# One layer of a hybrid decoder: the attention heads taken by pairs, on halves of TensorE's rows and columns

## The reference, cut to what matters

```
xn   = RMSNorm(x)
proj = xn @ w_in     -> q, k, v (8 heads of 64), index q (8 x 64), index k (64), index w (8), u (256), qm (4 x 64)
A    = sparse attention: index score = sum over 8 heads of relu(iq . ik / 8) * iw, causal;
       the 64 best keys of each query are kept; softmax(q . k / 8) over them, times v
B    = pooling mixer: causal windows 2, 4, 8, 16 over 4 groups of 64 channels, each group times its 64 x 64 weight
C    = cross-attention of qm (4 heads of 64) into 256 memory tokens
h    = x + (sum over branches of sigmoid(xn @ w_gate + b_gate) * (branch @ w_proj)) @ w_out
h    = h + MoE(RMSNorm(h)): the best 4 of 32 experts, clamped SwiGLU, 1024 -> 2048 -> 1024
out  = RMSNorm(h)
```

## Time and profile before

| | us |
|---|---|
| median of 3 runs (lowest, highest) | 1206.98 (1204.16, 1207.64) |
| profiled execution, its own time | 1203.21 |
| its span, first to last instruction | 1201.0 |
| PE busy in the span | 1121.9 (93%) |
| DVE busy | 359.7 (30%) |
| ACT busy | 227.3 (19%) |
| POOL busy | 128.6 (11%) |

### The profile page before, as it was taken

One profiled execution on the slowest core, in us unless ns is written; L12 is line 12 of the kernel. 1 busy time (PEld: TensorE's weight loads), 2 busy tenths in 40 slices (PEclk: granted clock), 3 DMA queues, 4 the chain that ended last, 5 costly groups with the idle time before them and its releaser, 6 DMA issues.

```text
span 1201.0 us, 14123 instructions
## 1 busy us (share of the span) xinstructions
PE 1121.9 (93%) x5609; PEld 510.0 (42%) x5609; DVE 359.7 (30%) x766; ACT 227.3 (19%) x415; POOL 128.6 (11%) x59
## 2 busy tenths in 40 slices
PE   6899999999999999999999989999989899989996
PEld 5788898753333333333333323333323233333332
DVE  4593664632222222122222222222212122222222
ACT  5354454121111111111111111111111111111112
POOL 5562666400000000000000000000000000000000
PEclk9999999989999999999999999999999999999999
DMA  9554335779999999999999999999999999999993
GB/s 355 194 177 145 113 141 188 276 310 403 384 428 427 428 427 426 427 427 430 427 427 427 427 427 427 428 428 427 429 428 427 427 427 427 427 427 427 428 426 142
DMA packets 50230, 444.22 MB, mean 370 GB/s; under 512 B 6094, under 2 KB 9592, under 8 KB 25592
## 3 DMA queue, kind: packets, MB, share of 16 engines
q1 hardware_dynamic: 48256, 441.64, 88.5%
q10 hardware_dynamic: 1912, 1.66, 0.5%
HBM read 441.65 MB, written 1.05 MB: 369 GB/s over the span
## 4 chain that ended last, share of the span: by engine, by line
PE 61%; DMA 28%; DVE 6%; ACT 3%; issue 1%; POOL 0%; SPq 0%; DVEq 0%; ACTq 0%
PE psum L1476 23%; PE psum L1512 14%; DMA ring<-in_w_up 14%; PE psum L1177 11%; DMA gm_area<-in_w_up 10%; DMA my_area<-in_w_up 4%; PE psum L1431 3%; PE psum L1364 2%; DVE gate_area L1110 1%; DVE gate_area L1114 1%; DVE gate_area L1108 1%; PE psum L1499 1%; ACT gate_area L770 1%; PE psum L1485 1%; PE psum L1220 1%
## 5 line engine op out<-in xcount | busy, mean ns | idle before, releaser
L1476 PE MATMUL psum<-ring,gate_area 128*64 128x512 f32 x1216 | 280.0, 604 | 21.7 <-DMA ring<-in_w_up 13.4
L1080 DVE TENSOR_TENSOR h_s<-psum,h_s 128x512 f32<-128x512 f32 x132 | 82.0, 684 | 426.0 <-PE psum L1431 426.0
L1476 PEld LDWEIGHTS psum<-ring,gate_area 128*64 128x64 f32 x1216 | 85.8, 139 | 203.9 <-issue 173.3
L1512 PE MATMUL psum<-ring,gate_area 128*64 128x512 f32 x640 | 145.8, 595 | 5.3 <-ACT gate_area L770 5.3
L535 POOL TENSOR_TENSOR unit_lo<-ring,unit_hi 128x1024 fp32r<-128x1024 f32 (+1 forms) x54 | 128.2, 2380 | 95.3 <-ACT unit_hi L568 95.2
L764 ACT ACTIVATE gate_area<-gate_area 128x512 f32<-128x512 f32 x32 | 20.1, 630 | 532.0 <-DVE gate_area L1106 532.0
L1106 DVE TENSOR_SCALAR gate_area<-psum 128x512 f32<-128x512 f32 x32 | 22.1, 692 | 277.1 <-PE psum L1485 277.1
L1512 PEld LDWEIGHTS psum<-ring,gate_area 128*64 128x64 f32 x640 | 44.3, 136 | 86.3 <-issue 76.3
L1476 PE MATMUL psum<-gm_area,gate_area 128*64 128x512 f32 x256 | 60.3, 609 | 6.4 <-DMA gm_area<-in_w_up 6.4
L1431 PE MATMUL psum<-pT_s,gate_area 64*128 64x512 f32 x264 | 65.6, 615 | 0.7 <-ACT pT_s L774 0.7
L568 ACT ACTIVATE unit_hi<-ring 128x1024 fp32r<-128x1024 f32 (+1 forms) x54 | 55.5, 1032 | 47.6 <-PE psum L1177 47.4
(11 more groups left out here) (244 smaller groups left out, 1180.3 us busy)
## 6 DMA issues: line engine op xcount, KB each, us to landing
ring<-in_w_up SPq DMA_DIRECT2D x76, 2048.0 KB, 37.1
ring<-in_w_down SPq DMA_DIRECT2D x40, 2048.0 KB, 38.2
qe_area<-in_w_up SPq DMA_DIRECT2D x16, 2048.0 KB, 36.8
gm_area<-in_w_up SPq DMA_DIRECT2D x16, 2048.0 KB, 39.9
my_area<-in_w_up SPq DMA_DIRECT2D x12, 2048.0 KB, 35.2
xv_area<-in_w_up SPq DMA_DIRECT2D x8, 2048.0 KB, 37.9
xv_area<-in_w_down SPq DMA_DIRECT2D x8, 2048.0 KB, 38.7
my_area<-in_w_down SPq DMA_DIRECT2D x8, 2048.0 KB, 43.6
```

Of the source, the lines that this page charges most:

```text
L1080: nc.vector.tensor_tensor(h_s[:, b, cols], psum[:, BACK_BANKS[j], :], h_s[:, b, cols], ALU.add).then_inc(added, 1)
L1476: ins = nc.tensor.matmul(psum[lo:lo + SLOTS, c, :], lhsT, w[:, at:at + 512], start=(k == 0), stop=False)
L1512: ins = nc.tensor.matmul(psum[c * SLOTS:(c + 1) * SLOTS, DOWN_BANK, :], lhsT, w[:, at:at + 512], start=(f == 0), stop=(f == KC - 1))
```

## The change

Two heads that share a tile of 128 partitions are now one pair. Their scores are two series of matmuls, one on rows 0 to 63, one on rows 64 to 127 of the array, alternating and writing different banks; the padded copies, their zeros, the half copies and the semaphore are gone. The values of a pair are multiplied alternating between column halves into one bank; so is pooling, in one job. The mix uses row half and column half g % 2 for group g. The loop goes over 6 pairs with four gates in each, with a new job list, and the constant weights of the mix come in two DMAs. `bias_parts` stands ahead of the softmax of the first pair. In the last pair attend stands ahead of the last gate.

```
-    for n in range(nh):
-        jobs += [(("gate", 2 * n), "act")]
-        jobs += [(("pT", n), "act")]
-        if n + 1 < nh:
-            jobs += [(("sc", n + 1), "act" if n + 1 < MHEADS else "dve")]
-        jobs += [(("gate", 2 * n + 1), "act"), (("o", n), "dve")]
+    jobs += [(("sc", n), "act") for n in range(2)]
+    for m in range(PAIRS):
+        jobs += [(("gate", 4 * m + i), "act") for i in range(2)]
+        jobs += [(("pT", 2 * m + i), "act") for i in range(2)]
+        if m + 1 < PAIRS:
+            jobs += [(("sc", 2 * m + 2 + i), "act" if m + 1 < MPAIRS else "dve") for i in range(2)]
+            jobs += [(("gate", 4 * m + 2 + i), "act") for i in range(2)] + [(("o", m), "dve")]
+        else:
+            jobs += [(("gate", 4 * m + 2), "act"), (("o", m), "dve"), (("gate", 4 * m + 3), "act")]
...
 ACT
-            act.wait_ge(zeros_set, 1)
-            copy_halves("ikT", ikT[:, :], ikT_odd, lambda t: t[:, 0:S])
+            copy("ikT", ikT, lambda t: t[:, 0:S])
...
-            copy_halves("kmT", kmT, kmT_odd, pair)
+            copy("kmT", kmT, pair)
...
-                copy_halves(("kT", j), kT[:, 2 * j:2 * j + 2, :], kT_odd[:, 2 * j:2 * j + 2, :], pair)
+                copy(("kT", j), kT[:, 2 * j:2 * j + 2, :], pair)
...
             exps(0)
-            for n in range(nh):
-                gate(2 * n)
-                copy_pT(n)
-                if n + 1 < nh:
-                    exps(n + 1)
-                gate(2 * n + 1)
+            exps(1)
+            for m in range(PAIRS):
+                gate(4 * m)
+                gate(4 * m + 1)
+                copy_pT(2 * m)
+                copy_pT(2 * m + 1)
+                if m + 1 < MPAIRS:
+                    exps(2 * m + 2)
+                    exps(2 * m + 3)
+                gate(4 * m + 2)
+                if MPAIRS <= m + 1 < PAIRS:
+                    exps(2 * m + 2)
+                    exps(2 * m + 3)
+                gate(4 * m + 3)
...
 DVE
-            maxima(0)
-            normalise(0)
-            for n in range(nh):
-                if n + 1 < nh:
-                    maxima(n + 1)
-                    normalise(n + 1)
-                take_o(n)
-                if n == 0:
-                    bias_parts()
+            bias_parts()
+            for n in range(2):
+                maxima(n)
+            for n in range(2):
+                normalise(n)
+            for m in range(PAIRS):
+                if m + 1 < PAIRS:
+                    for n in (2 * m + 2, 2 * m + 3):
+                        maxima(n)
+                    for n in (2 * m + 2, 2 * m + 3):
+                        normalise(n)
+                take_o(m)
...
 PE
             def causal_scores(t, qt, kt):
-                nc.tensor.matmul(t[:, 0:P], qt[:, 0:P], kt[:, 0:P], start=True, stop=True)
-                return nc.tensor.matmul(t[:, P:P + S], qt[:, P:S], kt[:, 0:S], start=True, stop=True)
+                parts = (slice(0, HD), slice(HD, P))
+                for i, part in enumerate(parts):
+                    nc.tensor.matmul(t[i][:, 0:P], qt[part, 0:P], kt[part, 0:P], start=True, stop=True)
+                for i, part in enumerate(parts):
+                    done(nc.tensor.matmul(t[i][:, P:P + S], qt[part, P:S], kt[part, 0:S], start=True, stop=True))
...
+            t = fill("pool")
+            for j in range(G // 2):
+                for b in range(B):
+                    for i in range(2):
+                        g = 2 * j + i
+                        ins = nc.tensor.matmul(t[i * HD:(i + 1) * HD, j * S:(j + 1) * S], u_s[:, b, g * HD:(g + 1) * HD],
                                                pool_a[:, b, g, :], start=(b == 0), stop=(b == B - 1))
...
+                part = slice(HD * (g % 2), HD * (g % 2 + 1))
+                ins = nc.tensor.matmul(t[part, (g // 2) * S:(g // 2 + 1) * S], wg_s[part, g // 2, :],
+                                       pooledT[part, g // 2, :], start=True, stop=True)
...
+            def attend(m):
+                t = fill(("o", m))
+                pe.wait_ge(act_emptied, EMPTIED["pT", 2 * m + 1])
+                for s in range(2):
+                    for i in range(2):
+                        part = slice(HD * i, HD * (i + 1))
+                        n = 2 * m + i
+                        if m < MPAIRS:
+                            v, cols = vm_s[:, s, n * HD:(n + 1) * HD], slice(0, S)
+                        else:
+                            v, cols = v_s[:, s, (n - MHEADS) * HD:(n - MHEADS + 1) * HD], slice(s * P, S)
+                        ins = nc.tensor.matmul(t[part, cols], v, pT_s[:, i, s * S:s * S + cols.stop - cols.start],
+                                               start=(s == 0), stop=(s == 1))
+                done(ins)
...
-            for n in range(nh):
-                gate(2 * n)
-                turn_p(n)
-                if n + 1 == MHEADS:
-                    pe.wait_ge(act_emptied, EMPTIED["kT", 1])
-                if n + 1 < nh:
-                    scores(n + 1)
-                gate(2 * n + 1)
-                attend(n)
+            for m in range(PAIRS):
+                gate(4 * m)
+                gate(4 * m + 1)
+                turn_p(2 * m)
+                turn_p(2 * m + 1)
+                if m + 1 == MPAIRS:
+                    pe.wait_ge(act_emptied, EMPTIED["kT", 1])
+                if m + 1 < PAIRS:
+                    scores(m + 1)
+                gate(4 * m + 2)
+                if m + 1 == PAIRS:
+                    attend(m)
+                gate(4 * m + 3)
+                if m + 1 < PAIRS:
+                    attend(m)
```

More of the change, by code:

```diff
@@ L32 @@
 MHEADS = 4
+MPAIRS = MHEADS // 2
+PAIRS = (MHEADS + HEADS) // 2
 HD = 64
@@ L56 @@
 GB = 2 * KC + 2
-N_CONST = 8
+N_CONST = 9
 RING_SLOTS = 4
@@ L115, in psum_jobs @@
     jobs += [(("idx", h), "act") for h in range(IHEADS)]
-    jobs += [(("pool", j), "dve") for j in range(2)]
+    jobs += [("pool", "dve")]
     jobs += [(("K", b), "act") for b in range(B)] + [("mix", "dve")]
@@ L609, in pair @@
                 return t.rearrange("p (c s) -> p c s", c=2)
-            def copy_halves(name, even, odd, part):
-                t = empty(name)
-                nc.scalar.activation(even[0:HD], part(t)[0:HD], ACT.Copy)
-                nc.scalar.activation(odd[HD:P], part(t)[HD:P], ACT.Copy).then_inc(act_emptied, 1)
             for b in range(B):
@@ L901, in take_top @@
                     link(nc.vector.tensor_tensor(bias[:, d], bias[:, d], causal[:], ALU.add))
-            for j in range(2):
-                t = empty(("pool", j))
-                nc.vector.tensor_copy(pooledT[0:HD, 2 * j:2 * j + 2, :],
-                                      t[0:HD, :].rearrange("p (g s) -> p g s", g=2)).then_inc(dve_emptied, 1)
+            t = empty("pool")
+            nc.vector.tensor_copy(pooledT, t.rearrange("p (g s) -> p g s", g=2)).then_inc(dve_emptied, 1)
             take_top(0, 0, TOPK // 8)
@@ L964, in normalise, with take_o @@
                 ins.then_inc(p_ready, 1)
-            def take_o(n):
-                t = empty(("o", n))
-                part = slice(HD * (n % 2), HD * (n % 2 + 1))
-                name, c = ("mem", n // 2) if n < MHEADS else ("attn", (n - MHEADS) // 2)
-                hi, lo = (y[part, c, :] for y in y_parts[name])
-                link(nc.vector.tensor_copy(hi, t[part, 0:S]))
-                nc.vector.tensor_tensor(lo, t[part, 0:S], hi.bitcast(F32), ALU.subtract).then_inc(dve_emptied, 1)
-            nh = MHEADS + HEADS
-            maxima(0)
-            normalise(0)
-            for n in range(nh):
-                if n + 1 < nh:
-                    maxima(n + 1)
-                    normalise(n + 1)
-                take_o(n)
-                if n == 0:
-                    bias_parts()
-                if n == 6:
+            def take_o(m):
+                t = empty(("o", m))
+                name, c = ("mem", m) if m < MPAIRS else ("attn", m - MPAIRS)
+                hi, lo = (y[:, c, :] for y in y_parts[name])
+                link(nc.vector.tensor_copy(hi, t[:, 0:S]))
+                nc.vector.tensor_tensor(lo, t[:, 0:S], hi.bitcast(F32), ALU.subtract).then_inc(dve_emptied, 1)
+            bias_parts()
[10 more added lines that the diff above has]
+                take_o(m)
+                if m == 3:
                     hi, lo = y_parts["pool"]
@@ new lines, in causal_scores @@
+                for i, part in enumerate(parts):
+                    nc.tensor.matmul(t[i][:, 0:P], qt[part, 0:P], kt[part, 0:P], start=True, stop=True)
+                for i, part in enumerate(parts):
+                    done(nc.tensor.matmul(t[i][:, P:P + S], qt[part, P:S], kt[part, 0:S], start=True, stop=True))
+            for c in range(IHEADS // 2):
+                t = [fill(("idx", 2 * c + i)) for i in range(2)]
+                causal_scores(t, iqT[:, c, :], ikT)
+            pe.wait_ge(got_const, 16 * N_CONST)
@@ L1238, in _ @@
             for g in range(G):
-                lo = HD * (g % 2)
```

(25 more changed lines are left out.)

57 lines of the change are left out of this document (10 added, 47 removed).

## The result

The changed kernel takes 1190.26 us (median of 4 runs, 1186.85 to 1190.39), the kernel before 1205.57 us (4 runs, 1202.53 to 1207.64): ratio 0.9873, 95% interval 0.9845 to 0.9901. The prediction was 1191 us, within 1185 to 1200. The profiled execution took 1190.39 us, its span is 1188.1 us: 12.9 us less than the one before.

What follows compares the result with a forecast made beforehand. PE bounds the front, DMA transfer the expert part. Terms 1.7 + 4.1 + 8.9 = 14.7 us give 1188.5 us from the profiled execution, 1192.3 from the median; forecast 1191, range 1185 to 1200.

Steps and rivals of the forecast that it cites:

- What bounds: Whole kernel: PE bounds the front, DMA transfer the expert part; a microsecond off PE's front moves the expert part equally.
- One sign of being wrong: Expert part: the prediction would be wrong if this part were longer than before by more than 2 us.
- Ahead of the loop: Index pairs and pooling save 3.7 us, but projection K waits for a bank and a unit; V 1.7 us earlier.
- The mix: Mix ahead of V: eight instructions stay at 1.01 us; by the skill's bank rule 1.76, 0.75 us more.
- Start of the loop and its end: Heads' loop: PE's waits of 0.86, 1.74, 0.56 and 0.98 us go; 4.1 us, ends 2.5 and 4.2.
- PE's work in the loop: Heads' loop: memory heads 2.9, attention heads 4.0, fewer change-overs 2.0 us; sum 8.9 us, pairs of 14.1 us.
- What could be late: Heads' loop: nothing late; slack 2.8 us for a pair's softmax, 2.4 us for units, banks long emptied.
- Rival 3: Doubled softmax: DVE instructions meeting POOL make every pair wait; slower, 1212 us at 4 us a pair; chance 0.05.
- Sum: Up to the branch projections: 1.7 + 4.1 + 8.9 = 14.7 us earlier, all behind moving with them.
- The ends of the terms: Each term's low and high values, from which the forecast's own range was made: gain 10 to 18 us.

Runs made afterwards that it cites:

- e4: Changed kernel with an unread full-array transpose between the two heads of each attention score, index score and value pair; 1198.31 us, ratio 0.9956.
- e10: Changed kernel with 28 extra DVE instructions in each pair, between the maxima and the divisions; 1218.89 us, ratio 1.012 to the kernel before.
- e0: The changed kernel run again with no edit; 1189.86 us, ratio 0.9872 to the kernel before.
- e3: Changed kernel with DVE's rotation of q moved behind the choice of the top keys; 1186.69 us, ratio 0.9855 to the kernel before.
- e5: Changed kernel with attend behind the last gate again in the last pair; 1192.19 us, ratio 0.9899 to the kernel before.
- e7: Kernel before with one edit, bias_parts ahead of the zeros and the first softmax; 1202.8 us, ratio 0.9992.
- e11: Changed kernel with bias_parts back behind the first take_o; 1189.73 us, ratio 0.9898 to the kernel before.
- e6: Changed kernel with 14 extra DVE instructions in each pair, between the maxima and the divisions; 1190.73 us, ratio 0.9887 to the kernel before.
- e2: Changed kernel with values and pooling issued one column half after the other; 1188.68 us, ratio 0.9876 to the kernel before.
- e1: Changed kernel with all scores of a pair issued head by head, one row half first; 1188.62 us, ratio 0.9867 to the kernel before.
- e8: Changed kernel with five unread full-array matmuls where PE idles between out-projection and first expert; 1185.59 us, ratio 0.9836 to the kernel before.
- e9: Changed kernel with both the later rotation of q and the five filler matmuls; 1182.77 us, ratio 0.982 to the kernel before.

## Why the prediction was right, point by point

**What bounds.** PE in the front, bytes in the expert part. Right: the rest lies between 920.2 and 924.3 us in all fourteen traces, whatever D is, and what e4 and e10 add to D (11.2 and 30.8 us) comes out in their times: their ratios of 0.9956 and 1.012 against e0's 0.9872 are 10.1 and 29.9 us. One sign of being wrong did show, though: from the first expert matmul to the end it was 926.4 us before and 928.6 after, 2.2 us longer where the prediction allowed 2. It lies in the first 16 expert matmuls at half clock; e0 has 926.0 us there.

**Ahead of the loop.** The term was 1.7 us of a possible 3.7, with K at 59.9, a late unit, V at 72.6. Measured 59.95, 68.77 for the unit, V at 72.72: 19.24 us from the first index score to V, where it was 21.04, 1.8 us less. e3 shows the cause: with DVE's rotation out of the way the wait for the bank and the wait for the unit both go, 1.87 us. It also shows that the loss was not needed.

**The mix.** 1.01 us by the chain before and 1.08 busy in both the earlier trace rows, as taken. The rule of the Trainium skill, "TensorEngine Tiling (Array Packing)", section "Restrictions and Gotchas", that different row tiles can't access one bank at once, would have made it 1.76 us. The measurement decides: it cost nothing here. The matmuls on the two row halves start two by two, 6 to 7 ns apart, and write one bank.

**Start of the loop and its end.** Put at 4.1 us, all four waits gone. All four are gone. e5 confirms one of them alone (0.96 us for 0.98). That the copies and the two gates beside the first softmax removed the waits of 0.86 and 1.74 us is read from the traces, no run tests it alone. The reason given for `bias_parts` was too narrow: e7 gives 0.76 us in the old order, and e11 shows that in the new order the place does not matter, where two heads' room for the softmax covers it (e6 found room for 5.4 us).

**PE's work in the loop.** Put at 8.9 us with a pair of 14.1; the pair measured 14.20, and 14.69 - 1.80 - 4.14 leaves 8.75 us for the term. The overlap of row halves, which no row had shown at these widths, is there, and e4 shows that it is the overlap which gives the gain. But the two parts of the term, 6.9 us of overlap and 2.0 us of fewer change-overs, were both off. A head before, from the chain that ended last, behind the first gate of the earlier trace rows: transposes, scores, a gate, values.

```profile
154.84 0.33 PE psum L1306 x3
155.17 0.22 PE psum L1219 x2
155.39 0.43 PE psum L1220 x2
155.83 2.86 PE psum L1177 x24
158.69 0.58 PE psum L1315 x2
159.27 0.22 PE psum L1320 x2
```

Two heads took 1.30 us for scores, 1.60 for values and 2 x (3.06 + 2.86) = 11.84 for gates; the pair takes 0.85, 0.80 and 11.89. The overlap is full: index pairs stand 0.65 us apart where one head took 0.66, which saves 0.65 us in a pair of scores and not 0.5. At the prediction's own prices (a gate 2.87, transposes 0.66, scores and values 0.65 each when fully overlapped) the 14.20 us leave 0.76 for change-overs, where two heads had 0.66 and the sum had taken 0.33. So the step that failed is that half as many change-overs cost half as much: going over to half rows and back costs some 0.2 us each time. Four L1210 behind the transposes take 0.42 us where two L1219 took 0.22, and two gates behind the scores take 5.94 us, 0.2 more than two of 2.87, where one gate behind the scores took 2.86. The overlap gave 0.3 us more a pair and the change-overs 0.4 us less, so the two errors nearly cancel.

**What could be late.** No wait came, right. The room at the end of the chain was sized well: 2.8 us were given for the softmax, and it was 2.5. What was wrong is that extra work adds to the chain in full: of e6's 5.4 us only 0.9 did, since the work first fills DVE's wait for the exponentials and moves the divisions away from POOL's subtraction. Rival 3's consequence, a softmax that comes late in every pair, exists: e10 has it, brought about by 10.8 us of extra work per pair and not by POOL. Work less room would make it 8 us of wait a pair; it was 3.8, and with what the lower clock took some 6, a cost that the rival had not counted.

**Sum.** D was to fall by 14.7 us and fell by 14.69. The three terms are each right to 0.2 us (1.7, 4.1 and 8.9 put, 1.80, 4.14 and 8.75 measured). That the last is so close is luck, since its two parts were off in opposite ways. The ends of the terms add up to 8.9 and 17.1 us, not to the 10 and 18 from which the range was made; nothing hung on it. What the sum left out is E: it let all behind move along unchanged, and E grew by 2.17 us in the profiled execution, because the half clock lasted 17.1 instead of 10.2 us. e0 has 10.2 us again with the same kernel, so this is a matter of the execution, not of the change. The sum's 1188.5 us for an execution like the profiled one stands against 1190.39, and its 1192.3 from the medians against 1190.26, and the 1191 was chosen between the two.

## What to carry to other kernels

Where a kernel has a compute-bound front and a transfer-bound rest, measure a front change between two milestones of the trace: here that was good to 0.05 us while whole times spread over 3 to 7 us. Before booking a saving on one engine, look who empties the banks and fills the operands of its next stage, since half of the first saving went into a bank that ACT emptied late, behind a job of DVE, and moving that one small job got it back. Count what stands between different kinds of matmul, too: taking the array by halves halved the time of the small matmuls here, while the changes to halves and back cost no less than the changes before. And look at idle stretches of TensorE for their clock as well as their length: five idle-time matmuls brought more (3.9 us in E against the same kernel with 10.2 us at half clock) than any of the waits removed.

## What the runs showed of the hardware that was not expected

**Halves overlap without being alternated.** Four instructions on one half followed by four on the other take the 1.02 us that alternating ones take (e2), and start two by two some 13 ns apart; one full-array instruction between them ends it (e4). The Trainium skill, "TensorE: Matmul & The Clock Gate", section "Step-by-step: what each phase is for", says that matmuls stay in program order and only weight loads are pulled ahead. By that, e2's pairs should have needed an estimated 1.5 us (at 0.22 us an instruction); the measurement differs. In e1 the first L1211 (54.886 us), whose half comes first in the program, starts behind the other half's first L1210 (54.575).

**The clock after waits.** In every trace without fillers TensorE's granted clock was 0.50 (1.2 GHz instead of 2.4) for 10.2 to 17.1 us in the stretch where PE does the router's small matmuls and waits between them; with fillers in those waits it was never below full there (e8, e9). In e10, with two waits of 1.5 to 2.3 us about 3 us apart in the midst of dense work in every pair, it fell five times, each time during the second wait or within 1.3 us of its end. The length of such a stretch differs between executions of one kernel (17.1 and 10.2 us in two profiles of the changed kernel).

**A slower engine that costs nothing.** 5.4 us of extra DVE work per pair left D unchanged to 0.01 us (e6), partly because the instructions that POOL had stretched to 2.77 us fell to 0.55 us when they came later, and partly because DVE had stood waiting for 1.60 us before.
